# Maximum pass of the prompt attention: the mask added by VectorE instead of TensorE, and two heads of 64 rows side by side

## What is computed

```python
sc = indexer_scores(qib, wib, ki, q_pos, k_pos)   # -inf above the diagonal
_, idx = lax.top_k(sc, 256)
valid = idx <= q_pos[None, :, None]
s = einsum('bqngd,bqknd->bqngk', qg, gather(k, idx)) * 64 ** -0.5   # 16 heads on 4 key heads, width 64
s = where(valid, s, -inf)
p = softmax(s); o = einsum('bqngk,bqknd->bqngd', p, gather(v, idx))
```

## Time and profile before

| | us |
|---|---|
| median of 3 runs | 6386.84 (6369.41 to 6388.28) |
| the profiled execution's own time | 6381.06 |
| its span, first to last instruction | 6379.3 |
| PE / DVE / ACT / POOL busy in the span | 4882.5 / 2275.0 / 1870.2 / 699.7 |
| maximum pass, first to last unit | 702.7 to 2806.8 |
| L812 on DVE, 640 instructions | 365.2 busy, idle before them 278.1 |
| L1007 / L1008 on PE, 640 each | 246.8 / 241.3 busy, PE idle before L1007 291.0 |

### The profile page before, as it was taken

How to read it: one execution, slowest core, us unless ns; L and a number is a source line. 1 busy time by engine, 2 the same in 40 slices (tenths; PEclk the granted TensorE clock), 3 DMA queues, 4 the chain that set the end, 5 groups by cost and what they waited for, 6 DMA issues and landing times. The chain is left out here.

```text
span 6379.3 us, 58455 instructions
## 1 busy us (share of the span) xinstructions
PE 4882.5 (77%) x16452; PEld 2506.2 (39%) x16453; DVE 2275.0 (36%) x5015; ACT 1870.2 (29%) x3244; POOL 699.7 (11%) x900
## 2 busy tenths in 40 slices
PE   7999356777889998887675599936888886569980
PEld 2444122223333333333234444415565564534440
DVE  1111464445445546643122310134444442331105
ACT  0111134455666552221121122212222231212222
POOL 0111210000000000111221000120000000200013
PEclk9999577788999999998885699967898896579995
DMA  6111100000000000005342677771100100437865
GB/s 241 57 50 41 49 19 12 12 12 12 5 12 12 12 12 12 17 14 196 110 137 97 260 280 283 256 285 50 40 20 20 39 13 12 157 124 256 303 236 201
DMA packets 177186, 634.11 MB, mean 99 GB/s; under 512 B 28920, under 2 KB 47737, under 8 KB 157930
## 3 DMA queue, kind: packets, MB, share of 16 engines
q1 hardware_dynamic: 116764, 425.22, 19.0%
q0 software_dynamic: 39072, 131.90, 5.9%
q10 hardware_dynamic: 21184, 75.03, 2.9%
HBM read 497.41 MB, written 134.72 MB: 99 GB/s over the span
## 5 line engine op out<-in xcount | busy, mean ns | idle before, releaser
L2142 PE MATMUL experts_ps_gu<-w_sb,experts_xT 128*128 x1504 | 679.3, 606 | 43.9 <-DMA w_sb<-moe_w_in 39.4
L997 PE MATMUL attend_po<-attend_PT,V 128*128 128x512 f32 x1088 | 572.1, 652 | 8.9 <-ACT attend_total L742 8.9
L2659 PE MATMUL recurrent_psAB<-recurrent_hT,rec_w_in_sb 128*128 128x256 f32 (+1 forms) x2304 | 537.4, 393 | 10.6 <-ACT recurrent_hT L2454 10.6
L769 ACT ACTIVATE attend_passed<-attend_score,attend_cand 128x1024 bf16<-128x1024 f32 (+8 forms) x279 | 439.4, 1575 | 357.1 <-DVE attend_cand L869 333.3
L469 PE MATMUL project_pj<-project_w,project_hT 128*128 128x512 f32 (+2 forms) x1360 | 507.4, 531 | 6.6 <-ACT project_proj L385 5.5
L2659 PEld LDWEIGHTS recurrent_psAB<-recurrent_hT,rec_w_in_sb 128*128 128x128 f32 x2304 | 465.2, 216 | 76.7 <-issue 11.7
L1007 PE MATMUL attend_aux<-attend_hide,attend_identb 128*128 128x512 bf16 (+3 forms) x640 | 246.8, 389 | 291.0 <-DVE attend_mx L812 241.1
L812 DVE TENSOR_REDUCE attend_mx<-attend_aux 128x1 f32<-128x512 f32 (+3 forms) x640 | 365.2, 606 | 278.1 <-PE attend_aux L1008 270.7
L2142 PEld LDWEIGHTS experts_ps_gu<-w_sb,experts_xT 128*128 128x128 f32 x1504 | 285.4, 195 | 372.7 <-issue 372.7
L732 ACT ACTIVATE attend_PT<-attend_big 128x512 f32<-128x512 f32 x544 | 292.2, 588 | 366.0 <-PE attend_big L986 365.3
L2132 PE MATMUL experts_ps_y<-w_sb,experts_midT 128*128 x752 | 342.9, 599 | 11.4 <-issue 11.4
(11 more groups left out here) (425 smaller groups left out, 6132.3 us busy)
## 6 DMA issues: line engine op xcount, KB each, us to landing
w_sb<-moe_w_in SPq DMA_DIRECT2D x64, 2048.0 KB, 11.4
w_sb<-moe_w_in SPq DMA_DIRECT2D x64, 1024.0 KB, 8.8
yb_scratch<-experts_y ACTq DMA_DIRECT2D x94, 512.0 KB, 8.6
index_slab<-ada_w_in SPq DMA_DIRECT2D x12, 2048.0 KB, 12.1
sample_V<-cache_v_in POOLq DMA_DIRECT2D x128, 128.0 KB, 2.4
sample_K<-cache_k_in SPq DMA_DIRECT2D x128, 128.0 KB
route_x<-xa_scratch SPq DMA_DIRECT2D x32, 512.0 KB, 4.6
hs_scratch<-route_h ACTq DMA_DIRECT2D x32, 512.0 KB, 4.8
```

The costliest lines, as they stand in the source:

```text
L769: act.activation(passed[:, 0:L[m]], score[:, m % 2, 0:L[m]], ACT.Sign, bias=threshold, accum_out=balance[:, :]).then_inc(balanced, 1)
L997: pe.matmul(po[:, n % 2, :], V1[:, b, n, :], PT[:, g % 4, :], start=(b == 0), stop=(b == S[i] // NKV - 1)).then_inc(pv_done, 1)
L2142: last = pe.matmul(ps_gu[:, u, :], xT[:, u, k, :], w1[:, bass.ds(slot, 1), k, :].rearrange("p a n -> p (a n)"), start=(k == 0), stop=(k == ...
L2659: last = pe.matmul(psAB[:, c % 2, part, 0:W], w_in[:, k, part * D + c * P:part * D + (c + 1) * P], hT[:, k, 0:W], start=(k == 0), stop=(k ...
```

## The change

Each unit now has one product, of 64 rows, and units go in pairs: the two heads of a pair have their rows at partitions 0 to 63 and 64 to 127. The mask is added by DVE, in one instruction that also takes the maximum and writes the sums to a scratch tile `junk`. `qTb` shrinks to 8 by 128 columns and is one cast of 128 partitions. A slot's share is counted in pairs, and PE's early part is half of the pairs, rounded down.

```diff
-        def units_at(i, s):
-            return share_of(U[i + 1], s, 0, max(middle(i), 1)) if there(i + 1) else range(0)
+        def unit_pairs_at(i, s):
+            return share_of(U[i + 1] // 2, s, 0, max(middle(i), 1)) if there(i + 1) else range(0)
+        def unit_pair(m, v):
+            jg, c = divmod(v, CUTS[m])
+            return jg // GQ, jg % GQ, c, slice(512 * c, min(512 * c + 512, L[m]))
...
-                    for r in range(2):
-                        pool.drain()
-                        pool.tensor_copy(qTb[r * DH:(r + 1) * DH, :, :]...[:, r],
-                                         qT[r * DH:(r + 1) * DH, m % 3]...).then_inc(qTb_ready, 1)
+                    pool.tensor_copy(qTb[:, :, :], qT[:, m % 3]).then_inc(qTb_ready, 1)
...
                 def largest(m, u):
-                    h, c = divmod(u, CUTS[m])
-                    wide = min(512, L[m] - 512 * c)
+                    j, g, c, keys = unit_pair(m, u // 2)
+                    h = (2 * j + u % 2) * GQ + g
+                    wide = keys.stop - keys.start
+                    if u == 0:
+                        dve.wait_ge(hidden, m + 1)
                     dve.wait_ge(unit_filled, sum(U[:m]) + u + 1)
-                    dve.tensor_reduce(mx[:, h, c:c + 1], aux[:, u % 2, 0:wide], AX.X, ALU.max).then_inc(maxed, 1)
+                    dve.wait_ge(maxed, sum(U[:m]) + u + 1)
+                    dve.tensor_tensor_reduce(junk[:, u % 2, 0:wide], aux[:, u % 2, 0:wide], hide[:, keys], 1.0, LOWEST,
+                                             ALU.add, ALU.max, mx[:, h, c:c + 1]).then_inc(maxed, 1)
...
-                def fill(m, u):
-                    h, c = divmod(u, CUTS[m])
...
-                    pe.wait_ge(maxed, sum(U[:m]) + u + 1)
-                    pe.matmul(aux[:, u % 2, 0:n], identb4[:, 0, :], hide[:, keys], start=True, stop=False)
-                    pe.matmul(aux[:, u % 2, 0:n], qTb[:, h, :], KTb[:, h // GQ // 2, keys], start=False, stop=True).then_inc(unit_filled, 1)
+                def fill(m, v):
+                    j, g, c, keys = unit_pair(m, v)
+                    if v == 0:
+                        pe.wait_ge(qTb_ready, m + 1)
+                    for half in range(2):
+                        r = rows_of_half(half)
+                        pe.wait_ge(maxed, sum(U[:m]) + 2 * v + half + 1)
+                        pe.matmul(aux[:, half, 0:keys.stop - keys.start], qTb[r, j * GQ + g, :], KTb[r, j, keys],
+                                  start=True, stop=True).then_inc(unit_filled, 1)
...
-                        units, pairs = units_at(i, s), pairs_at(i, s)
+                        units, pairs = unit_pairs_at(i, s), pairs_at(i, s)
```

More of the change, by code:

```diff
@@ L55 @@
 MASKED = -1.0e30
-TAKEN = -3.0e38
 BIG = 1.0e30
+LOWEST = -3.0e38
 class Semaphores:
@@ L509, in phase_attend @@
         qT = sb("qT", [P, 3, H // 2, P])
-        qTb = sb("qTb", [P, H, P], BF16)
+        qTb = sb("qTb", [P, H // 2, P], BF16)
         qiT = sb("qiT", [P, IH // 2, P])
@@ L524, in phase_attend @@
         othermax = sb("othermax", [P, H])
+        junk = sb("junk", [P, 2, 512], BF16)
         mx = sb("mx", [P, H, 4])
@@ L661, in _ @@
                     pool.tensor_copy(KTb[:, n, :], KT[:, n, :]).then_inc(consts, 1)
-                pool.memset(qTb[:, :, :], 0.0).then_inc(consts, 1)
                 for half in range(2):
@@ L665, in _ @@
                     pool.memset(half_hide[rows_of_half(1 - half), :, half, :], 1.0).then_inc(consts, 1)
-                pool.wait_ge(consts, 7 + GQ)
+                pool.wait_ge(consts, 6 + GQ)
                 for half in range(2):
@@ L671, in _ @@
                                          identb4[rows_of_half(half), 0:1, half * DH:half * DH + DH].broadcast_to([DH, H, DH])).then_inc(consts, 1)
-                pool.wait_ge(consts, 11 + GQ)
+                pool.wait_ge(consts, 10 + GQ)
                 def split_hide(m):
@@ L706, in narrow @@
                     pool.wait_ge(qT_ready, 4 * (m + 1))
-                    for r in range(2):
-                        pool.drain()
-                        pool.tensor_copy(qTb[r * DH:(r + 1) * DH, :, :].rearrange("p (j r g) q -> p r j (g q)", r=2, g=GQ)[:, r],
-                                         qT[r * DH:(r + 1) * DH, m % 3].rearrange("p (j g) q -> p j (g q)", g=GQ)).then_inc(qTb_ready, 1)
+                    pool.tensor_copy(qTb[:, :, :], qT[:, m % 3]).then_inc(qTb_ready, 1)
                 for i in steps():
@@ L723, in _ @@
                 act.sem_inc(exped, 4)
-                act.wait_ge(consts, 11 + GQ)
+                act.wait_ge(consts, 10 + GQ)
                 def exponentials(i, s):
@@ L805, in _ @@
                 dve.sem_inc(summed, 4)
-                dve.wait_ge(consts, 11 + GQ)
+                dve.wait_ge(consts, 10 + GQ)
                 def largest(m, u):
-                    h, c = divmod(u, CUTS[m])
-                    wide = min(512, L[m] - 512 * c)
+                    j, g, c, keys = unit_pair(m, u // 2)
[3 more added lines that the diff above has]
+                        dve.wait_ge(hidden, m + 1)
                     dve.wait_ge(unit_filled, sum(U[:m]) + u + 1)
-                    dve.tensor_reduce(mx[:, h, c:c + 1], aux[:, u % 2, 0:wide], AX.X, ALU.max).then_inc(maxed, 1)
+                    dve.wait_ge(maxed, sum(U[:m]) + u + 1)
+                    dve.tensor_tensor_reduce(junk[:, u % 2, 0:wide], aux[:, u % 2, 0:wide], hide[:, keys], 1.0, LOWEST,
+                                             ALU.add, ALU.max, mx[:, h, c:c + 1]).then_inc(maxed, 1)
                     if u == U[m] - 1:
@@ L923, in finish_search @@
                                 dve.wait_ge(split_done, 2 * m)
-                                dve.wait_ge(unit_filled, sum(U[:m]))
+                            dve.drain()
                             dve.memset(out, 0.0)
@@ L948, in _ @@
                     for s in range(slots(i)):
-                        for u in units_at(i, s):
-                            largest(i + 1, u)
+                        for v in unit_pairs_at(i, s):
+                            largest(i + 1, 2 * v)
+                            largest(i + 1, 2 * v + 1)
                         if there(i - 1):
@@ L964, in _ @@
                 pe.sem_inc(pv_done, 4)
-                pe.wait_ge(consts, 11 + GQ)
+                pe.wait_ge(consts, 10 + GQ)
                 def place_of(i, k):
@@ L997, in with_values @@
                     pe.matmul(po[:, n % 2, :], V1[:, b, n, :], PT[:, g % 4, :], start=(b == 0), stop=(b == S[i] // NKV - 1)).then_inc(pv_done, 1)
-                def fill(m, u):
-                    h, c = divmod(u, CUTS[m])
-                    n = min(512, L[m] - 512 * c)
-                    keys = slice(512 * c, 512 * c + n)
-                    if u == 0:
-                        pe.wait_ge(qTb_ready, 2 * (m + 1))
-                        pe.wait_ge(hidden, m + 1)
-                    pe.wait_ge(maxed, sum(U[:m]) + u + 1)
-                    pe.matmul(aux[:, u % 2, 0:n], identb4[:, 0, :], hide[:, keys], start=True, stop=False)
-                    pe.matmul(aux[:, u % 2, 0:n], qTb[:, h, :], KTb[:, h // GQ // 2, keys], start=False, stop=True).then_inc(unit_filled, 1)
+                def fill(m, v):
[7 more added lines that the diff above has]
+                                  start=True, stop=True).then_inc(unit_filled, 1)
                 def project(i):
```

## The result

| | before | after |
|---|---|---|
| median (lowest to highest), 4 runs each | 6385.18 us (6369.41 to 6388.28) | 6280.56 us (6279.82 to 6283.89) |
| profiled execution, its span | 6381.06, 6379.3 | 6279.82, 6278.3 |
| first PE instruction behind the attention | 2929.4 | 2837.2 |
| PE / DVE / ACT / POOL busy | 4882.5 / 2275.0 / 1870.2 / 699.7 | 4795.1 / 2274.6 / 1870.1 / 685.3 |

The ratio is 0.9842, with an interval of 0.9825 to 0.9859: 1.6% faster, 105 us where 30 to 36 were predicted, and under the range's lower end of 6290. Of it 92 us are won by the end of the attention. What stands behind the attention is the same code. In the profiled executions of the 18 kernels of this study it took from 3441 to 3452 us, 3450 before and 3441 after, so the last 9 us are of the size by which executions differ. For small effects I therefore read where the attention ends, beside the median.

A forecast was written before the change was run, and what follows sets the result against it. It took a chain through in-order DVE (PE's units, maxima, search rounds waiting for ACT) to bound most first halves of attention steps. Terms summed to -34; 4 kept back gave -30, 6381.06 to 6351, range 6290 to 6415.

The forecast's parts named there:

- A: Maxima on DVE: the new instruction's accumulator read and semaphore wait put units 0.80 us apart against 0.66; +90 us.
- B: DVE's short waits for a bank inside slots: one product of half the time refills always in time; -40 us.
- D: DVE's other waits of 1 us and more, for PV or PE's own chain, get 0.6 shorter each; -19 us.
- C: PV between maxima, tiles 7, 5, 11: with one pair ahead, PE does PV while DVE searches; -41 us.
- E: Step start: PE's first unit waits for one POOL cast of 1.1 us instead of two, 2.21; -20 us.
- F: Two 64-row products side by side on PE: a pair 0.22 us instead of 0.86; counted only in tile 4's step, -4.
- R3: PE's order sets the slots, DVE-PE waits are slack: -205, 6176, chance 0.02; halfway -80, 6300, chance 0.14.
- R1: Tiles 10, 8, 6 and search-filled slots: DVE pays +0.20 a unit in full, +42, 6423; chance 0.11, extreme 6620 0.03.
- R2: PE idles more between units, its granted clock falls towards 0.77, PV slows: +50, 6400; chance 0.20 together with R4.
- R4: Nothing moves: A near its upper end, B to E as forecast, about 0; chance 0.20 together with R2.

The follow-up runs named there:

- after_plain_reduce: The changed kernel with a plain maximum in place of the one that adds the mask, the mask left out of that pass; 6279.88 us, 0.9847.
- mask_on_dve: The kernel before with only the mask moved to DVE's maximum instruction; 128-row padded products, two casts and old order stay; 6351.93 us, 0.9965.
- before_order_in_pairs: The kernel before with only a slot's shares counted in pairs and a whole number of pairs ahead of PV; 6335.43 us, 0.9936.
- one_pair_ahead: The changed kernel with at most one pair of units ahead of PV, the other pairs behind it; 6268.21 us, 0.9825.
- mask_on_dve_in_pairs: The kernel before with mask on DVE and order in pairs; products still 128 padded rows, two casts; 6298.88 us, 0.9871.
- after_products_twice: The changed kernel with each 64-row product made twice into the same bank, results the same; 6334.11 us, 0.9928.
- one_pair_cast_by_columns: The changed kernel with at most one pair ahead of PV and POOL's cast split by columns, PE's first pair waiting for the first part; 6259.30 us, 0.9816.
- pairs_mask_in_turn: The kernel before with 64-row pairs, one cast and pair order, the mask staying on PE, mask and 64-row product bank by bank; 6387.06 us, 1.0013.

## Why the prediction was wrong

| step | predicted | what the runs show |
|---|---|---|
| A, dearer unit on DVE | +90 | about 0 (after_plain_reduce: 1 us apart, 9 in the attention) |
| B and D, less PE work before a unit | -40, -19 | -25 alone (mask_on_dve); -37 on top of C |
| C, order in pairs | -41 | -42 alone; 49 lost when taken out of the changed kernel |
| E, one cast | -20 | 40 lost when taken out; -13 for the short wait where products are padded |
| F, 64-row pairs | -4 | 0 with a short step start, +22 with the long one |
| sum | -34 | -105 |

*The step that failed is A.* Its first part, "0.61 + 0.08", took the accumulator read as time ahead of the next unit, from rows in which the next instruction needs the count. For independent units it lies beside the next one. Its second part, "in addition the new unit waits for its predecessor's semaphore" (+0.11), was misread from the code: the wait is for `maxed` at sum + u + 1, and `maxed` starts at 2, so unit u waits for unit u - 2, since `junk` has two halves. That one has long been done. With A at 0 the other terms as predicted give -124, 19 beyond the measured 105: the rest was somewhat too hopeful. The range's lower end had A at no less than +51, so an A of 0 lay outside all cases but R3.

*B and D* have the right sign and about half the size. With the mask alone moved, DVE's waits before units fell by 36 us in all where B and D had 59: those under 1 us from 49 to 20 (B had 40 of them go), those of 1 us and more inside slots from 110 to 100 (D had 19 go), and the first ones of the steps grew by 3. Of the 36, 28 show in the attention.

*C* was right in mechanism, place (in before_order_in_pairs the halves of tiles 5, 7 and 11 won 5, 21 and 7 us of the 40) and size. It had missed that in tiles 1 and 3 two pairs still stand ahead of PV, with waits of 3.3 to 3.8 us, which is where one_pair_ahead gains.

*E* was right on the row (POOL's cast is 1.03 us), and DVE's 16 first waits of a step fell by the forecast 20, from 111.5 to 92.0 us. Taking it out cost more, 34 us in the attention: 20 of it is PE's wait and 10 the slower PV behind it. Shortening the wait further won only its own length. Why the wait for the second cast costs 40 us with 64-row products and 13 with padded ones (34 and 18 in the attention) is open: the gap is more than the runs scatter, and no run changes the clock alone.

*F* put 0.22 for a bf16 pair and counted no row changes, on the ground that PE had room. By the rows a pair is 0.32, and PV between two such pairs takes 0.21 more, so that 0.14 of 0.44 us are left in a slot with two pairs. F had the price of a change right (0.1 to 0.2), and its slot of about 4.1 us in tile 15's step too (0.53 of biases and 3.51). The Trainium skill states in TensorEngine Tiling ("Key Properties") that changing the tiling mode drains the engine; the time that these traces show at each change agrees with it.

*The rivals.* R1 fell: units are 0.61 apart. The Trainium skill's halving of throughput (Vector Engine (DVE) Microarchitecture Reference, "Points that are easy to get wrong") did not appear with one source in PSUM and a bf16 one, at 689 ns for 512 elements; by the letter of that entry of the skill it would not. R2 did not decide: the granted clock is 0.95 in tile 15's half (0.97 before) and 0.77 in tile 7's, as before. It did fall over the attention as a whole, from 0.88 to 0.86, and as far with the mask alone moved; what that cost is not separated. R4 fell.

R3 has the number that lies closest, -80 at its halfway case, but that is luck. It has PE's work set the slots, with DVE's waits as slack. mask_on_dve takes 640 products off PE, of 0.22 us each for 512 keys at the full clock, so some 120 us in all by the number of keys (an estimate), and 28 reached the end. What moves with the attention is DVE's wait for its units. Against the kernel before, wait and attention fell by 36 and 28 in mask_on_dve, 42 and 40 in before_order_in_pairs, 88 and 81 in mask_on_dve_in_pairs, and 102 and 92 in the changed kernel. PE's time counts where it makes DVE wait, as in after_products_twice (45 and 52 more than in the changed kernel).

The best version is one_pair_cast_by_columns, 6259.3 us: 21 under the change as made, 1.8% under the kernel before.

## What to carry to other kernels

Read what follows an accumulator read before pricing it: here the next unit, which did not need the result, started beside the read. What a semaphore's wait names, with its starting value, decides whether it can bind at all. Price work taken off one engine by the waits that it ends on the engine that carries the chain, not by the work itself. With n banks between a producer and a consumer, put at most n units ahead of a long piece of other work in the producer's queue, since the next one ties that work to the consumer. Price half-height products with the neighbours in the queue: here the changes of row count took two thirds of what lying side by side saved.

## What the hardware showed that I had not expected

- One instruction with an addition, a maximum over 512 elements, a bf16 copy of the sums and an accumulator result takes DVE no longer than the plain maximum: 689 ns against 687, and 0.61 us from start to start in a row.
- A drain between two such instructions costs 0.21 us (0.82 to 0.83 apart), of which 0.15 reached the end here.
- POOL casts 128 partitions by 1024 elements in 1.03 us, as long as one of its casts of 64 partitions by 1024 (1.03 each; two with a drain between them take 2.21).
- A change between 128 and 64 rows on PE cost 0.10 us between bf16 products. PV's four fp32 products take 1.72 us between neighbours of 128 rows, 1.82 behind a 64-row one, and 1.92 with 64 rows on both sides (medians of 57, 59 and 20 places at the full clock, in before, pairs_mask_in_turn and after).
